# A deeper expert ring and channel-half spectral products in a two-layer hybrid trunk

## What is computed

```python
def hyena(u, short_w, short_b, kf, hy_d):            # one of the four head groups, 256 channels
    u = depthwise_conv(u, short_w, short_b)
    v, x1, x2 = jnp.split(u, 3, axis=-1)
    z = v.astype(jnp.float32)
    for o, gate in enumerate((x1, x2)):               # two orders
        zf = jnp.fft.rfft(z, n=2 * L, axis=1)
        y = jnp.fft.irfft(zf * kf[None, :, o, :], n=2 * L, axis=1)[:, :L]
        z = gate.astype(jnp.float32) * (y + hy_d[o].astype(jnp.float32) * z)
    return z.astype(u.dtype)

def run(args):                                        # one expert on its tokens, 32 experts, top 2 per token
    tok, e = args
    xb = t[tok]
    return (jax.nn.silu(xb @ e_gate[e]) * (xb @ e_up[e])) @ e_down[e]
```

## Time and profile before

| what | us |
|---|---|
| median of three runs | 1599.42 (1596.72 to 1603.11) |
| the profiled execution | 1598.85 |
| its span (first to last instruction) | 1597.0 |
| TensorE matmul busy | 1261.4 (79%) |
| VectorE busy | 544.6 (34%) |
| ACT busy | 380.8 (24%) |
| GpSimd busy | 260.0 (16%) |

### The profile page before, as it was taken

The page is one execution under the profiler, slowest core; times in us unless marked ns, Lnnn a source line. Parts: engine busy times, 40 slices in busy tenths (PEclk is TensorE's granted clock), DMA queues, the critical chain, the costliest instruction groups (busy, mean ns, idle before and its releaser), DMA issues.

```text
span 1597.0 us, 16657 instructions
## 1 busy us (share of the span) xinstructions
PE 1261.4 (79%) x6542; PEld 734.6 (46%) x6542; DVE 544.6 (34%) x1136; ACT 380.8 (24%) x739; POOL 260.0 (16%) x273
## 2 busy tenths in 40 slices
PE   3899988877997688988783899797699587777770
PEld 1455464444344444655442466544555444444430
DVE  3327455354124332221004274654523500000006
ACT  4311124310223122222115211332023221111123
POOL 4210110002000123232220016000000022222220
PEclk9899999988998799999996899999799689999995
DMA  9647220064555599999996021102100579999974
GB/s 352 246 141 285 107 77 27 27 198 155 202 174 213 207 416 418 396 413 375 394 414 266 1 79 27 50 27 86 60 1 40 211 303 418 411 412 407 396 293 202
DMA packets 73232, 356.36 MB, mean 223 GB/s; under 512 B 13165, under 2 KB 21995, under 8 KB 37704
## 3 DMA queue, kind: packets, MB, share of 16 engines
q1 hardware_dynamic: 57724, 322.25, 52.3%
q0 software_dynamic: 12704, 22.03, 3.8%
q10 hardware_dynamic: 2732, 11.08, 1.8%
HBM read 338.23 MB, written 31.23 MB: 231 GB/s over the span
## 4 chain that ended last, share of the span: by engine, by line
PE 55%; DMA 23%; DVE 11%; ACT 5%; issue 3%; SPq 1%; ACTq 0%; POOL 0%; POOLq 0%; DVEq 0%
DMA ring<-in_exp_up 19%; PE ps L1305 10%; PE ps L1253 9%; PE ps L1100 5%; PE ps L1010 4%; PE ps L1061 3%; PE ps L1320 3%; PE ps L871 3%; PE ps L1031 2%; PE ps L1210 2%; DMA ring<-in_ada_w 1%; PE ps L924 1%; PE ps L1233 1%; DMA work<-y_scratch 1%; DMA work<-h_scratch,tabs 1%
## 5 line engine op out<-in xcount | busy, mean ns | idle before, releaser
L1305 PE MATMUL ps<-ring,work 128*64 128x256 f32 x2176 | 254.8, 387 | 48.2 <-DMA ring<-in_exp_up 45.0
L1305 PEld LDWEIGHTS ps<-ring,work 128*64 128x64 f32 x2176 | 173.6, 139 | 154.2 <-issue 97.5
L1320 PE MATMUL ps<-ring,work 128*64 128x512 f32 x544 | 134.6, 616 | 26.1 <-DVE work L2177 21.5
L1253 PE MATMUL ps<-ring,yT 128*128 128x512 f32 x320 | 146.4, 608 | 2.0 <-DVE yT L2038 2.0
L2175 DVE TENSOR_TENSOR work<-work,ps 64x256 f32<-64x256 f32 x56 | 23.8, 425 | 344.6 <-ACT work L1669 344.6
L807 POOL DMA_INDIRECT y_scratch<-work,tabs x56 | 57.6, 1028 | 338.5 <-ACT work L1676 338.5
L1917 DVE SCALAR_TENSOR_TENSOR work<-work,prmT 128x655 f32<-128x655 f32 x120 | 97.7, 895 | 0.0
L1253 PEld LDWEIGHTS ps<-ring,yT 128*128 128x128 f32 x320 | 59.8, 194 | 76.4 <-issue 74.2
L802 POOL DMA_INDIRECT work<-h_scratch,tabs x60 | 61.7, 1028 | 173.1 <-DVE tabs L2163 147.4
L1100 PE MATMUL ps<-hT,ring 128*128 128x512 f32 x192 | 88.6, 604 | 1.1 <-DVE ring L1932 1.1
L1010 PE MATMUL ps<-hT,ring 128*128 128x512 f32 x128 | 69.5, 626 | 3.4 <-POOL hT L768 1.9
(11 more groups left out here) (369 smaller groups left out, 1759.6 us busy)
## 6 DMA issues: line engine op xcount, KB each, us to landing
ring<-in_exp_gate SPq DMA_DIRECT2D x68, 1024.0 KB, 8.2
ring<-in_exp_up SPq DMA_DIRECT2D x68, 1024.0 KB, 12.7
ring<-in_exp_down SPq DMA_DIRECT2D x68, 1024.0 KB, 11.9
ring<-in_ada_w SPq DMA_DIRECT2D x48, 1024.0 KB, 4.8
ring<-in_w_in SPq DMA_DIRECT2D x16, 1024.0 KB, 8.3
work<-y_scratch SPq DMA_DIRECT2D x8, 1024.0 KB, 7.9
ring<-in_w_out SPq DMA_DIRECT2D x6, 1024.0 KB, 4.9
k_scratch<-yT ACTq DMA_DIRECT2D x4, 1280.0 KB, 9.8
```

The lines of the kernel that those rows point to most:

```text
L1253: last = mm(ps[:, (4, 6, 7, 0)[n % 4], :], yT[:, k, t * P:(t + 1) * P], wo[k // 2][:, k % 2, h * HALF:(h + 1) * HALF], start=(k == 0), sto ...
L1305: last = mm(ps[BR * q:BR * q + BR, 1, 0:FE], xe[:, s, kb, BR * h:BR * h + BR], w[:, q, k, :], start=(k == 0), stop=(k == KC - 1))
L1320: last = mm(ps[BR * h:BR * h + BR, 3, :], he[:, s, k, :], wd[:, k, HALF * h:HALF * h + HALF], start=(k == 0), stop=(k == 1))
```

## The change

Two parts. The expert ring gets more units: `units` 6, 7 and 8 are the tables `inv_s`, `mix_s` and `fwd_s`, 9 and 10 the first 2 MB of `hT`, whose last part takes `nfb`; layer 0 uses three gate and up pairs and two down units, layer 1 four pairs and three downs. Loads run three (four) experts ahead for gate and up, two (three) for down. Because layer 0 overwrites them, `mix_s` and `inv_s` are loaded again at the start of layer 1. The counted loop keeps two slots.

In the Hyena part GpSimd's sums go, and VectorE works by channel half c, then by frequency half f, sum and difference in one instruction; the inverse of c waits for that half alone.

```diff
+        cprod = work[:, 5120:7168].rearrange("p (f r s q c) -> p f r s q c", f=2, r=2, s=2, q=2)
...
-        nfb = at(hflat, 0, D)
+        nfb = at(hflat, 2 * UNIT, D)
+        units = [ring[:, i, :] for i in range(6)] + [v.rearrange("p q t -> p (q t)") for v in (inv_s, mix_s, fwd_s)] \
+            + [hflat[:, i * UNIT:(i + 1) * UNIT] for i in range(2)]
+        gu_units = [[(0, 1), (3, 4), (6, 7)], [(0, 1), (3, 4), (6, 7), (9, 10)]]
+        dn_units = [[2, 5], [2, 5, 8]]
...
                 in_unit(l, 2)
                 in_unit(l, 3)
+                if l > 0:
+                    table(mix_s, "mix_s", tab_in)
+                    table(inv_s, "inv_s", tab_in)
...
-                sp.wait_ge(hy_y0, nth(l, hy_y0, 1))
-                sp.wait_ge(hy_y, nth(l, hy_y, 2))
+                sp.wait_ge(hy_y, nth(l, hy_y, 3))
                 spectra(l, 1)
...
+                def gate_up_in(n, e, done):
+                    g, u_ = gu_units[l][gu_slot(l, n)]
+                    sp.dma_start(units[g], gate[e]).then_inc(done, 16)
+                    sp.dma_start(units[u_], up[e]).then_inc(done, 16)
...
-                for n in range(NSTAT + SLOTS):
-                    s = n % SLOTS
-                    if n == 0:
-                        sp.wait_ge(wo_mm, nth(l, wo_mm, 10))
-                    elif n == 1:
-                        sp.wait_ge(a_used, 24 * DEPTH)
-                    else:
-                        if n == 2:
-                            gate_rows(l, 1, g2b)
-                        sp.wait_ge(g_mm, nth(l, g_mm, n - 1))
...
-                    expert(s, gate[l * NE + n], up[l * NE + n], wg_full[s] if n < NSTAT else d_wg[s])
-                    if n >= SLOTS:
-                        sp.wait_ge(y_mm, nth(l, y_mm, n - 1))
-                    sp.dma_start(ring[:, 3 * s + 2, :], down[l * NE + n]).then_inc(wd_full[s] if n < NSTAT else d_wd[s], 16)
+                ahead_g, ahead_d = len(gu_units[l]), len(dn_units[l])
+                sp.wait_ge(hy_inv, nth(l, hy_inv, 4))
+                gate_up_next(2)
+                if l:
+                    down_next(2)
+                sp.wait_ge(wo_mm, nth(l, wo_mm, 10))
+                gate_up_next(0)
+                down_next(0)
+                sp.wait_ge(a_used, 24 * DEPTH)
+                gate_up_next(1)
+                down_next(1)
+                gate_rows(l, 1, g2b)
+                if l:
+                    sp.wait_ge(hs_mm, nth(l, hs_mm, 10))
+                    gate_up_next(3)
+                for n in range(NSTAT + SLOTS - ahead_d):
+                    if n + ahead_d == NSTAT and l > 0:
+                        sp.wait_ge(over_clear, l)
+                    if n + ahead_g < NSTAT + SLOTS:
+                        sp.wait_ge(g_mm, nth(l, g_mm, n + 1))
+                        gate_up_next(n + ahead_g)
+                    sp.wait_ge(y_mm, nth(l, y_mm, n + 1))
+                    down_next(n + ahead_d)
...
-                for o in range(2):
-                    pool.wait_ge(hy_yp, nth(l, hy_yp, o + 1))
-                    pool.tensor_tensor(yspec[:, :, 0, :], zpm[:, 0, 0, :, :], zpm[:, 0, 1, :, :], ALU.add)
-                    pool.tensor_tensor(yspec[:, :, 2, :], zpm[:, 0, 0, :, :], zpm[:, 0, 1, :, :], ALU.subtract) \
-                        .then_inc(hy_y0, 1)
...
-                pe.wait_ge(tab_in, 112)
+                pe.wait_ge(tab_in, 112 + 32 * l)
...
-                                if c == 0 and e == 0:
-                                    if f == 0:
-                                        pe.wait_ge(hy_y0, nth(l, hy_y0, o + 1))
-                                    else:
-                                        pe.wait_ge(hy_y, nth(l, hy_y, 2 * o + 2))
+                                if e == 0 and f == 0:
+                                    pe.wait_ge(hy_y, nth(l, hy_y, 3 * o + 2 + c))
...
-                    for f in range(2):
-                        dve.wait_ge(hy_ez, nth(l, hy_ez, 2 * o + f + 1))
...
-                        V.tensor_tensor(zpm[:, f, 0, :, :], ez[:, f, :, :], odd, ALU.add)
-                        step(V.tensor_tensor(zpm[:, f, 1, :, :], ez[:, f, :, :], odd, ALU.subtract))
-                        times(zpm[:, f, 0, :, :], f, 1, zpm[:, f, 0, 0, :], zpm[:, f, 0, 1, :])
-                        last = times(zpm[:, f, 1, :, :], 2 + f, 0, zpm[:, f, 1, 0, :], zpm[:, f, 1, 1, :])
...
+                    for c in range(2):
+                        cs = slice(c * P, (c + 1) * P)
+                        for f in range(2):
+                            if c == 0:
+                                dve.wait_ge(hy_ez, nth(l, hy_ez, 2 * o + f + 1))
+                            odd = ps[:, 2 * f + 1, :].rearrange("p (q c) -> p q c", q=2)[:, :, cs]
+                            V.tensor_tensor(zpm[:, f, 0, :, cs], ez[:, f, :, cs], odd, ALU.add)
+                            step(V.tensor_tensor(zpm[:, f, 1, :, cs], ez[:, f, :, cs], odd, ALU.subtract))
+                            for r in range(2):
+                                k4 = kspec[:, r, f:4:2, cs].rearrange("p s (a c) -> p s a c", a=1).to_broadcast([P, 2, 2, P])
+                                last = V.tensor_tensor(cprod[:, f, r, :, :, :], zpm[:, f, :, :, cs], k4, ALU.mult)
+                            step(last)
+                            V.tensor_tensor(zpm[:, f, :, 0, cs], cprod[:, f, 0, :, 0, :], cprod[:, f, 1, :, 1, :], ALU.subtract)
+                            last = V.tensor_tensor(zpm[:, f, :, 1, cs], cprod[:, f, 0, :, 1, :], cprod[:, f, 1, :, 0, :], ALU.add)
+                        step(last)
+                        plus, minus = [zpm[:, :, q, :, cs].rearrange("p f q c -> p q f c") for q in range(2)]
+                        V.tensor_tensor(yspec[:, :, 0:2, cs], plus, minus, ALU.add)
+                        V.tensor_tensor(yspec[:, :, 2:4, cs], plus, minus, ALU.subtract).then_inc(hy_y, 1)
```

More of the change, by code:

```diff
@@ L409, in trunk @@
         ro_w = sem("ro_w")
-        wg_full = [sem(f"wg_full{s}") for s in range(SLOTS)]
         wd_full = [sem(f"wd_full{s}") for s in range(SLOTS)]
@@ L482, in w_count, with uses, gu_slot, dn_slot @@
         def w_count(l, j):
-            return 16 * (2 + 3 * l + j // 4) + 16 * ((j % 4 == 3) * l + (j == OUT_U + 3))
+            return 16 * (2 + 3 * l + j // 4) + 16 * ((j % 4 == 3) * l + (j == OUT_U + 3)) + l * 32 * uses(0, gu_units, j % 4, NSTAT)
+        def uses(l, slots, q, n):
+            return len([i for i in range(n) if i % len(slots[l]) == q])
+        def gu_slot(l, n):
+            return n % len(gu_units[l])
+        def dn_slot(l, n):
+            return n % len(dn_units[l])
+        def gu_sem(l, n):
+            return w_full[gu_slot(l, n)]
+        def dn_sem(l, n):
+            return (wd_full + a_full[:1])[dn_slot(l, n)]
+        def gu_count(l, n):
+            q = gu_slot(l, n)
+            return w_count(l, OUT_U + q) + 32 * uses(l, gu_units, q, n + 1)
+        def dn_count(l, n):
+            q = dn_slot(l, n)
+            earlier = 16 * l * uses(0, dn_units, q, NSTAT) if q < SLOTS else 16 * apos.count(4)
+            return earlier + 16 * uses(l, dn_units, q, n + 1)
         apos = [(4, 5, 0, 1, 2, 3)[p] if p < 6 else 4 if 24 <= p < 32 else 4 + p % 2 for p in range(24 * DEPTH)]
@@ L647, in _, with down_in, gate_up_next, down_next @@
                         ada_piece(p)
-                def expert(s, src_g, src_u, done):
-                    sp.dma_start(ring[:, 3 * s, :], src_g).then_inc(done, 16)
-                    sp.dma_start(ring[:, 3 * s + 1, :], src_u).then_inc(done, 16)
+                def gate_up_in(n, e, done):
+                    g, u_ = gu_units[l][gu_slot(l, n)]
+                    sp.dma_start(units[g], gate[e]).then_inc(done, 16)
+                    sp.dma_start(units[u_], up[e]).then_inc(done, 16)
+                def down_in(n, e, done):
+                    sp.dma_start(units[dn_units[l][dn_slot(l, n)]], down[e]).then_inc(done, 16)
+                def gate_up_next(n):
+                    gate_up_in(n, l * NE + n, gu_sem(l, n) if n < NSTAT else d_wg[n % SLOTS])
+                def down_next(n):
+                    down_in(n, l * NE + n, dn_sem(l, n) if n < NSTAT else d_wd[n % SLOTS])
                 gate = io["exp_gate"].rearrange("l e (p k) f -> (l e) p (k f)", k=KC)
@@ L678, in _ @@
                         sp.wait_ge(d_g, j * SLOTS + (s - 1))
-                        expert(s, gate[l * NE + e], up[l * NE + e], d_wg[s])
+                        gate_up_in(NSTAT + s, l * NE + e, d_wg[s])
                         sp.wait_ge(d_y, j * SLOTS + (s - 1))
-                        sp.dma_start(ring[:, 3 * s + 2, :], down[l * NE + e]).then_inc(d_wd[s], 16)
+                        down_in(NSTAT + s, l * NE + e, d_wd[s])
                 if l + 1 == DEPTH:
@@ L1297, in rows_in, with gate_up @@
                     return last
-                def gate_up(s):
-                    w = ring[:, 3 * s:3 * s + 2, :].rearrange("p q (k f) -> p q k f", k=KC)
+                def gate_up(s, n):
```

(5 more changed lines are left out.)

46 lines of the change are left out of this document (15 added, 31 removed).

## The result

The changed kernel takes 1574.49 us in the median of four runs (1571.71 to 1579.45), the kernel before 1600.35 beside it: a ratio of 0.9842, 95% interval 0.9816 to 0.9868, a gain of 25.9 us where 30.6 were forecast. A second set of runs gave 1575.61 us and 0.9862 (0.9829 to 0.9895), a gain of 23.4 us. The profiled execution took 1572.67 us (span 1570.8). Of the eight executions in the two sets, four, the two profiled ones among them, have a mean granted clock of 0.913 or 0.914 and take 1569.1 to 1572.7 us, and four have 0.908 to 0.912 and take 1576.3 to 1580.5.

What follows compares the result with a forecast made beforehand. It took DMA to bound both expert loops, with VectorE then TensorE in turn bounding the spectral products. Terms -12.5, -5.0, -7.0 and -6.1 sum to -30.6 from 1598.85, giving 1568 us, range 1558 to 1583.

Steps and rivals of the forecast that it cites:

- Ring, layer 1: Layer 1's expert loop: five transfers, 5.24 MB, loaded before the DMA-bound stretch save 12.5 us.
- Ring, layer 0: Layer 0's expert loop: one gate and up pair, 2 MB, loaded early saves 5.0 us.
- rival (d): Layer 0's expert loop: the larger ring fills DMA dips, a third of 20 us back, 1561 us; chance 0.04.
- The moved wait: Expert loop: the new load order moves the wait from L1305 to L1320 and costs nothing, 0 us.
- Reload of mix_s and inv_s: Start of layer 1: two 1 MB transfers on SP's queue cost 0 us, or 5 if their cover were gone.
- Products, layer 1: Layer 1's spectral products: TensorE starts its first half earlier, saving 3.5 us per order, 7.0 in all.
- the upper price: Spectral products: a half-width instruction costs as much as a full one, 9.1 us per half, 0.9 slower per order.
- Products, layer 0: Layer 0's spectral products among conditioning pieces: 6.1 us saved over both orders, between 0 and 8.
- The term for the conditioning pieces: Layer 0's Hyena part: pieces behind the first half move 4.6 us earlier; matmuls gain 1.5 in order 0, 4.6 in order 1.
- (a): Inverse's second half runs at the low clock after TensorE's pause, every order's gain gone, 1581 us; chance 0.10.
- (b): End of the fixed expert loop: two pairs left, DMA dry 5 us in each layer, 1578 us; chance 0.10.
- (c): Expert loops: gathers become the bound above a 10.2 us landing, slower at 1622 us; chance 0.05.

Runs made afterwards that it cites:

- alone: Changed kernel with the old spectral products, keeping only the deeper expert ring; ratio 0.9894 to the kernel before.
- late: Changed kernel with all its slots, but the additional slots' first loads issued only after expert 0's gate and up matmuls; ratio 0.9921 to the kernel before.
- ring of 3 and 2: Changed kernel with layer 1's ring cut to three gate and up pairs and two downs; ratio 0.9872 to the kernel before.
- fourth down: Changed kernel with one more down slot in layer 1, in the work tile, loaded before the loop; ratio 0.9791 to the kernel before.
- downs ahead: Changed kernel with the same units as two pairs and four downs in layer 0, three and five in layer 1; ratio 0.9875 to the kernel before.
- the kernels with the clock restored: Two variants of the changed kernel with four pairs and four downs in layer 1; that layer's loop stretch took 297.2 and 296.0 us.
- the products alone: Kernel before with only the new spectral products, its ring and loads as they were; ratio 0.9904 to the kernel before.
- the tail run: Changed kernel with loads of experts 30 and 31 issued in the fixed part; loop stretches 342.4 us in layer 0, 297.9 in layer 1.
- the second profile: Changed kernel run again, unchanged; ratio 0.9862 to the kernel before, layer 1's loop stretch 300.1 us.

## Why the prediction was right, and which terms were off

The time is inside the range and the direction is right; it gains 4.7 us less than the sum said, in the second set 7.2. The loops and the products together give 29.1 and 32.8 us in the two profiles against 30.6. Part of that closeness is luck: the ring's term for layer 0 was too small, and those for the products were too large.

- **Ring, layer 1, -12.5**: measured -12.7, -11.5 and, alone, -12.5. That each preloaded byte counts by its transfer time is shown by the stretches of three kernels (late: all of it lost; ring of 3 and 2: 7.0 to 8.1 for 7.5; fourth down: 1.8 and 2.9 for 2.5). It is not the whole rule: with downs ahead the same bytes came early and the loop was 2.4 to 3.5 us longer.
- **Ring, layer 0, -5.0**: measured -7.2, -8.9 and, alone, -6.4. The term was too small: it counted the bytes of the pair alone, and depth by itself fills dips there (4 to 6 us), which was rival (d).
- **The moved wait, 0**: right in time. Its side effect was not forecast: granted clock 0.95. The Trainium skill, TensorE: Matmul & The Clock Gate (HAM oscillation), describes a loop of short bursts of matmuls in which each wait for a DMA sends the clock back and the next burst starts slow. The 724 ns against 605 behind the waits of L1358 agree; the kernel before, with 26 such waits and granted 1.00, does not. DMA sets the pace in most of that loop (413 GB/s to 1490 us), and the kernels with the clock restored gained 1.6 us at most by it.
- **Reload of mix_s and inv_s, 0**: "between" moved by -0.4 and +1.1. `mix_s` landed 12.5 us after its issue at 861.3, and its first matmul came at 938.6.
- **Products, layer 1, -7.0**: 3.33 and, by the same rows of order 1, 3.19 us per order (1129.05 to 1148.48 against 1139.48 to 1162.10), 6.5 in all. VectorE's prices were right to a tenth: half one 8.3 us behind the copy (8.2 forecast), all done after 15.2 (15.2). The rest up to the stretch's -4.7 is the slower transform shown above. Of the bounds, the upper price comes to 0.2 us slower per order by the same rows and not 0.9 (0.6 us of it fall into VectorE's wait for the second copy), so that even this end, with nothing from layer 0, is 1582 and within the range.
- **Products, layer 0, -6.1**: measured -4.5 and -6.0. The term for the conditioning pieces was mis-sized: the first half of the inverse was given 5.8 us, partly at full clock; it runs 6.4 to 6.7, in layer 1 at granted 0.50 and 0.58, so the pieces behind it move less than 4.6 us. In order 1 it is 3.2 (matmul 388.77, 21.26 us behind order 1's copy, against 24.50), in order 0, with the spectrum in front, 1.1 and not 1.5 (353.91, 23.50 behind the copy, against 24.56).
- **Rivals**: (a) fell: the second halves have granted 1.00 and take 3.67 us. In the changed kernel the slow first half fills the pause that (a) needs; with the products alone TensorE did pause 1.15 us ahead of one second half (layer 1, order 1), and it took 3.72 us at granted 1.00. (b): the dry stretch is there, 7.4 us of DMA at 418 GB/s, but in layer 1 it costs 1 to 3 us and not 5, as TensorE is the next bound; layer 0's (slices 31 to 33 above) cost nothing that the tail run shows. (c) fell: no landing above 8.8 us in layer 1, and an earlier gather changes nothing. Layer 0 does have a landing of 10.7 us, above the 10.2 that (c) names, but the kernel before has 11.4 there. The Trainium skill, DMA: Bandwidth & Descriptors (Queues, rings and completion order), has each engine take turns between the queue rows; down loads now land after 20.3 to 21.7 us (medians of layer 1's loop) instead of 12.1, gathers after 7.3 instead of 7.4, which agrees.

What stays open: the timed medians gain 23 to 26 us and the profiles 26 to 30. A transform that is slow in some profiles and not in others is one place where executions of the same program differ; the rest of that difference is not traced. The timed lead of the fourth down over the second set (8.6 us) is larger than its loop explains (2.4 us); its clock is 0.921 to 0.924, so the clock may be behind it, but downs ahead, with the same clock and a pair less, shows no such lead.

## What to carry to other kernels

When a loop is bound by a full DMA stream, count the bytes that are in the chip before it starts; more slots by themselves bought time here only where the stream would otherwise have paused. A gap in the stream is no loss until one has looked whether its consumer waits. When a sum is split into halves for overlap, the gain is the shorter of the two pieces of work laid side by side, less what the split adds (here 6.0 us of TensorE less 2.2 of VectorE, 3.6 measured).

## What the runs showed that I had not expected

Where a wait stands in the expert goes with what TensorE's clock does. The waits for loads in layer 1's loop (us in total, times, longest), before and after:

```profile
PE ps L1305 <- DMA ring<-in_exp_up: 32.3, 26, 1.8
...
PE ps L1358 <- issue: 13.0, 7, 2.5
```

In the kernel before, 26 waits of up to 1.8 us stood ahead of 32 gate and up matmuls, and layer 1's loop kept granted 1.00; after, 7 waits of up to 2.5 us stand ahead of eight down matmuls, and it has 0.95. The length of the waits alone is not the reason: in the second profile six of up to 2.1 us ahead of downs go with 0.94, and with downs ahead 16 of up to 2.1 us ahead of gate and up go with 0.99. What else it hangs on is open. And the first, uninterrupted half of the inverse kept granted 0.50 for most of its 6.67 us, after 4.93 us in which TensorE had waited.
